# Splitting 640 tokens as 512 and 128 instead of 320 and 320 in the matmuls of a two-layer streaming encoder

## The chip, the core and the metric

The kernel runs on one core of one Trainium2 chip. The metric is device time in microseconds (us) of one launch. The inputs lie in the chip's main memory (HBM) at the start and the outputs lie there at the end.

## What is computed

Two layers of an encoder trunk, for 512 prompt tokens and, with the same weights, for 128 stream tokens (8 streams of 16). All data is float32. Cut to what matters:

```
def half_ffn(x, norms, w_gu, w_down):
    h = rms_norm(x, norms[0])
    g, u = jnp.split(h @ w_gu, 2, axis=-1)
    return x + 0.5 * rms_norm((jax.nn.silu(g) * u) @ w_down, norms[1])
...
def trunk_layer(x, past, ...):
    x = half_ffn(x, norm_ffn1, ffn1_w_gate_up, ffn1_w_down)
    m, st = token_mixer(rms_norm(x, norm_mix[0]), past, w_in, w_out, ...)
    x = x + rms_norm(m, norm_mix[1])
    x = half_ffn(x, norm_ffn2, ffn2_w_gate_up, ffn2_w_down)
```

The model width is 1024 and the hidden width of each FFN 2816. `token_mixer` holds a projection `h @ w_in`, sparse attention, a gated recurrence, a convolution, and a projection `mix @ w_out`. The change touches only the matmuls with the large weights (`w_gu`, `w_down`, `w_in`, `w_out`), the sum of squares behind `rms_norm`, and the instructions that read their results.

## The kernel before

**Layout.** Activations lie with channels on the 128 partitions and all 640 tokens along the free axis: tokens 0 to 511 are the prompt, 512 to 639 the streams. `x`, `y`, `hr`, `hid` and `proj` are cut into pieces of 128 channels by 640 tokens.

**A product in three.** Each float32 operand of a large matmul is split into a high part, rounded to the type `float32r`, and the rest, also `float32r`. `three` (L287 to L292) then issues three matmuls into one PSUM region, high times high, high weights times low activations, and low weights times high activations. Every matmul brings its own load of 128 x 128 weights into TensorE, so each matmul has one LDWEIGHTS. All of them show in the profile as L291.

**Two token parts.** A PSUM bank holds 512 float32 per partition, so 640 tokens need two. `product_tile` calls `three` twice: bank `4j+2c` takes tokens 0 to 319 and bank `4j+2c+1` tokens 320 to 639 (`HALF` is 320). `j` is 0 or 1 and alternates, so one half of the eight banks is filled while the other is read.

**The stages.** For each layer: `ffn` (first), `projections`, a mixer (`select_and_recur`, `attend`) that the change doesn't touch, `output_projection`, and `ffn` (second). `pair_of_tiles` computes two tiles of 128 output channels over 8 pieces of input channels, which is 8 x 2 x 2 x 3 = 96 matmuls; in `ffn` `down_tile` computes one tile over 12 or 10 pieces. A `Lead` opens each `ffn` and `projections`: DVE scales and adds the preceding result to `x` and splits it (L387, L384, L407), piece by piece. The first `pair_of_tiles` waits for each of the 8 pieces (`split`), with 12 matmuls to a piece. `ones_sum` (L316) adds squares over the channels by a matmul in plain float32 against a matrix of ones.

**What runs beside.** SP loads the weights into `stage` (L270), ACT rounds the high part into `wr` (L282), DVE subtracts for the low part (L286). DVE reads the PSUM results (L548, L550 for gate and up; L563, L565 for down; L621, L622, L626, L627 and L630 for the projection; L692 for the output projection). Each such read covers both banks as a view of 2 x 320 elements; `halves` gives its counterpart in SBUF the same shape. Semaphores join the engines: `w_lo` says that weights are ready, `evac` that PSUM has been read, `used` that a tile is complete.

Of the kernel before, what the change touches and what calls it, by code (L numbers as in the profile page):

```python
# [22 lines left out]
ALU = mybir.AluOpType  # L23
# [5 lines left out]
TOK = SEQ + NS * LS  # L29
# [34 lines left out]
def build(nc, ins, outs):  # L64
    stack = ExitStack()
    with stack:
# [5 lines left out]
        def sem(name, once=False):  # L72

            s = stack.enter_context(nc.semaphore(name))
            if not once:
                all_sems.append(s)
            return s
# [75 lines left out]
        def halves(view):  # L153

            return view.rearrange("p (a n) -> p a n", a=2)

        stored = sem("stored")
        par_in = sem("par_in")

# [134 lines left out]
        def product_tile(pe, j, k, c, width, size, v, start, stop):  # L294

            at_ = k * size + 128 * c
            for a in range(2):
                mm = three(pe, ps[:, 4 * j + 2 * c + a, 0:HALF], lambda s: wr[:, j, s, at_:at_ + 128],
                           lambda t: v[:, t, k, a * HALF:(a + 1) * HALF], start, stop)
            return mm  # L300

        def pair_of_tiles(pe, i, j, n0, width=2, split=None):
# [10 lines left out]
        def ones_sum(pe, bank, view, done):  # L313

            for a in range(2):
                mm = pe.matmul(ps[:, bank + a, 0:HALF], ones[:], view[:, a * HALF:(a + 1) * HALF],  # L316
                               start=True, stop=True)
            mm.then_inc(done, 1)

        class Lead:  # L320
# [48 lines left out]

            def act_norm(self, act):  # L370
                act.wait_ge(self.total, 1)
                act.activation(halves(rs), ps[:, 4:6, 0:HALF], ACT.Sqrt, bias=EPS, scale=1.0 / D).then_inc(self.root, 1)

            def pool_part(self, pool):
                pool.wait_ge(self.y_total, 1)
# [43 lines left out]
        def ffn(l, tag, n0, wgu, wd, lead, first, after, ahead):  # L419
# [17 lines left out]
            with nc.Block() as block:  # L437
# [92 lines left out]
                @block.vector  # L530
                def _(dve):
                    if n0 == 0:
                        dve.wait_ge(par_in, 16)
                        dve.wait_ge(x_in, 16)
                        dve.sem_inc(evac, 2)
                        split_lo(dve, 0, 0, 0)
                    lead.dve_part(dve)
                    lead.dve_norm(dve)
                    rs2 = halves(rs)
                    if n0 == 0:  # L540
                        dve.wait_ge(table_out, 16)
                    dve.sem_inc(hid_ready, 1)
                    for f0, nf, gu, dn in chunks:
                        with dve.Fori(0, nf // 2) as i:
                            for j in range(2):
                                dve.wait_ge(used, i * 2 + (gu + j + 1))
                                dve.wait_ge(hid_ready, i * 2 + (f0 + j + 1))
                                dve.tensor_tensor(halves(sg[:, 0]), ps[:, 4 * j:4 * j + 2, 0:HALF], rs2,  # L548
                                                  ALU.mult).then_inc(g_scaled, 1)
                                dve.tensor_tensor(halves(sg[:, 1]), ps[:, 4 * j + 2:4 * j + 4, 0:HALF], rs2,  # L550
                                                  ALU.mult).then_inc(evac, 1)
                                dve.wait_ge(evac, i * 2 + (gu + j + 3))
                                dve.wait_ge(silu, i * 2 + (f0 + j + 1))
                                dve.tensor_tensor(sg[:, 1], sg[:, 0], sg[:, 1], ALU.mult).then_inc(hid_done, 1)  # L554
                                dve.wait_ge(hid_hi, i * 2 + (f0 + j + 1))
                                dve.tensor_tensor(hid_view(i, j, 1), sg[:, 1], hid_view(i, j, 0).bitcast(F32),  # L556
                                                  ALU.subtract).then_inc(hid_ready, 1)
                                split_lo(dve, i, j, gu + 2)
                        def down_tile(i, j, split):
                            dve.wait_ge(used, i * 2 + (dn + j + 1))  # L560
                            src = ps[:, 4 * j:4 * j + 2, 0:HALF]
                            if f0 == 0:
                                dve.tensor_copy(halves(yv[:, i, j, :]), src).then_inc(evac, 1)  # L563
                            else:
                                dve.tensor_tensor(halves(yv[:, i, j, :]), halves(yv[:, i, j, :]), src,  # L565
                                                  ALU.add).then_inc(evac, 1)
                            if split:
                                split_lo(dve, i, j, dn + 2)
                        last = bool(f0)
                        with dve.Fori(0, KD // 2 - last) as i:  # L570
                            for j in range(2):
                                down_tile(i, j, True)
                        if last:
                            down_tile(KD // 2 - 1, 0, ahead)
                            down_tile(KD // 2 - 1, 1, False)


        def projections(l, lead):
            w = ins["w_in"].rearrange("l (i j) p n -> l i j p n", j=2)
            pv = proj[:].rearrange("p (i j c) n -> p i j c n", j=2, c=2)  # L580
            NU = 12

            with nc.Block() as block:
                @block.sync
                def _(sp):
                    load_pairs(sp, PROJ + 2, NU - 2, lambda i, j: w[l, i + 1, j])

                @block.tensor
                def _(pe):
                    lead.pe_start(pe)  # L590
                    pair_of_tiles(pe, 0, 0, PROJ, split=lead.split)
                    lead.pe_norm(pe)
                    pair_of_tiles(pe, 0, 1, PROJ)
                    with pe.Fori(0, NU // 2 - 2) as i:
                        for j in range(2):
                            pair_of_tiles(pe, i, j, PROJ + 2)
                    for j in range(2):
                        pair_of_tiles(pe, NU // 2 - 1, j, PROJ, 2 - j)

                @block.scalar  # L600
                def _(act):
                    lead.act_part(act)
                    lead.act_norm(act)
                    with act.Fori(0, NU // 2 - 1) as i:
                        for j in range(2):
                            act.wait_ge(used, i * 2 + (PROJ + j + 1))
                            split_hi(act, i, j, PROJ + 2)

                @block.gpsimd
                def _(pool):  # L610
                    lead.pool_part(pool)

                @block.vector
                def _(dve):
                    lead.dve_part(dve)
                    lead.dve_norm(dve)
                    rs2 = halves(rs)
                    with dve.Fori(0, NU // 2 - 1) as i:
                        for j in range(2):
                            dve.wait_ge(used, i * 2 + (PROJ + j + 1))  # L620
                            dve.tensor_tensor(halves(pv[:, i, j, 0, :]), ps[:, 4 * j:4 * j + 2, 0:HALF], rs2, ALU.mult)  # L621
                            dve.tensor_tensor(halves(pv[:, i, j, 1, :]), ps[:, 4 * j + 2:4 * j + 4, 0:HALF], rs2,  # L622
                                              ALU.mult).then_inc(evac, 1)
                            split_lo(dve, i, j, PROJ + 2)
                    dve.wait_ge(used, OUTP - 1)
                    dve.tensor_tensor(halves(pv[:, NU // 2 - 1, 0, 0, :]), ps[:, 0:2, 0:HALF], rs2, ALU.mult)  # L626
                    dve.tensor_tensor(halves(pv[:, NU // 2 - 1, 0, 1, :]), ps[:, 2:4, 0:HALF], rs2,  # L627
                                      ALU.mult).then_inc(evac, 1)
                    dve.wait_ge(used, OUTP)
                    dve.tensor_tensor(halves(pv[:, NU // 2 - 1, 1, 0, :]), ps[:, 4:6, 0:HALF], rs2,  # L630
                                      ALU.mult).then_inc(evac, 1)


        def output_projection(l):
# [4 lines left out]
            with nc.Block() as block:  # L639
# [40 lines left out]
                def _(dve):  # L680
# [7 lines left out]
                    for s in range(4):  # L688
                        dve.wait_ge(used, OUTP + s + 1)
                        j = s % 2  # L690
                        for c in range(2):
                            cp = dve.tensor_copy(halves(y[:, 2 * s + c]), ps[:, 4 * j + 2 * c:4 * j + 2 * c + 2, 0:HALF])  # L692
                        cp.then_inc(evac, 1)
                        if s < 3:
                            split_lo(dve, s // 2, s % 2, OUTP + 2)
# [1022 lines left out]
```

## Time and profile before

| | us |
|---|---|
| time of three executions, median | 3253.17 |
| lowest, highest | 3252.92, 3257.25 |
| span of the profiled execution | 3254.3 |
| PE (matmuls) busy | 2851.5 |
| PEld (weight loads) busy | 2665.5 |
| DVE busy | 1528.1 |
| ACT busy | 944.0 |
| POOL busy | 476.2 |

The profiled execution has no time of its own beside its span. The span lies within the range of the three times and 1.1 us above their median, so a difference worked out on the span is applied to either alike. PE and PEld are the same engine, TensorE: matmuls and weight loads overlap, and their mean durations overlap with those of their neighbours too. So "mean ns" of one matmul is its latency, and what one costs in a stream is busy time divided by count. A plain float32 matmul stands in the trace as two records, each with a load.

### The profile page before, as it was taken

What the parts mean: (1) busy time and instruction counts of PE and PEld (TensorE: products, weight loads), DVE (VectorE), ACT (ScalarE), POOL (GpSimd) and SP (SyncE); (2) the same over time, 40 slices, a digit from 0 to 9 for tenths busy, and PEclk for the clock granted to TensorE, in tenths of its full rate; (3) what the DMA queues carried; (4) which work ended last, traced back from release to release, by engine and by line L of the source; (5) the groups of instructions that cost most, each with busy time, mean ns of one, the idle gap of its engine ahead of it and who ended that gap; (6) DMA issues with size and microseconds to landing.
All of it is one profiled execution on the core that took longest, in us unless ns stands there. A gap on an engine that the chain in (4) does not pass through costs nothing. (4 is left out here: it accounts for less than half of the span.)

```text
span 3254.3 us, 44093 instructions
## 1 busy us (share of the span) xinstructions
PE 2851.5 (88%) x18054; PEld 2665.5 (82%) x18054; DVE 1528.1 (47%) x1886; ACT 944.0 (29%) x1237; POOL 476.2 (15%) x328
## 2 busy tenths in 40 slices
PE   1999998997477979999969999989955788999997
PEld 1899998894354879999969999979834458999997
DVE  1633333528965353333353333352499644433333
ACT  1322223216423332212232212231362342322221
POOL 1100001105812120000120000020084313000001
PEclk9999999998768989999989999999976798999998
DMA  5122212113010212122112122122120111212211
GB/s 108 65 71 71 78 63 79 65 52 98 1 73 7 72 52 78 59 83 73 57 60 84 62 81 77 57 73 78 36 76 15 59 46 46 78 68 75 78 61 63
DMA packets 50676, 209.51 MB, mean 64 GB/s; under 512 B 13928, under 2 KB 14312, under 8 KB 34568
## 3 DMA queue, kind: packets, MB, share of 16 engines
q1 hardware_dynamic: 50568, 208.05, 19.3%
q8 instruction: 70, 1.15, 0.1%
q14 instruction: 38, 0.31, 0.0%
HBM read 197.85 MB, written 10.19 MB: 64 GB/s over the span
## 5 line engine op out<-in xcount | busy, mean ns | idle before, releaser
L291 PE MATMUL ps<-hr,wr 128*128 128x320 f32 x11424 | 1707.5, 311 | 83.6 <-DVE hr L407 65.7
L291 PEld LDWEIGHTS ps<-hr,wr 128*128 128x128 f32 x11424 | 1692.3, 189 | 99.7 <-DVE hr L407 43.5
L291 PE MATMUL ps<-hid,wr 128*128 128x320 f32 x4224 | 620.8, 309 | 0.0
L291 PEld LDWEIGHTS ps<-hid,wr 128*128 128x128 f32 x4224 | 619.8, 188 | 0.0
L286 DVE TENSOR_TENSOR wr<-stage,wr 128x2048 fp32r<-128x2048 f32 x184 | 421.7, 2292 | 299.7 <-ACT wr L282 299.7
L282 ACT ACTIVATE wr<-stage 128x2048 fp32r<-128x2048 f32 x184 | 350.6, 1905 | 557.5 <-PE ps L291 288.9
L548 DVE TENSOR_TENSOR arena<-ps,arena 128x640 f32<-128x640 f32 x88 | 72.5, 824 | 545.5 <-PE ps L291 543.8
L523 POOL TENSOR_TENSOR arena<-arena 128x640 f32<-128x640 f32 x28 | 44.3, 1582 | 1737.0 <-ACT arena L499 1737.0
L490 ACT ACTIVATE arena<-arena 128x640 f32<-128x640 f32 x88 | 65.1, 739 | 801.8 <-DVE arena L548 801.8
L860 POOL TENSOR_TENSOR proj<-proj,arena 128x640 f32<-128x640 f32 x120 | 200.1, 1669 | 33.6 <-ACT arena L1018 16.9
L938 PE MATMUL ps<-proj 128*128 128x256 f32 x264 | 90.9, 519 | 97.5 <-issue 78.4
L938 PEld LDWEIGHTS ps<-proj 128*128 128x128 f32 x264 | 70.2, 273 | 117.5 <-issue 82.1
L556 DVE TENSOR_TENSOR hid<-arena,hid 128x640 f32 x88 | 72.6, 825 | 91.8 <-ACT hid L492 91.8
L1017 ACT ACTIVATE arena<-arena,par 128x512 f32<-128x512 f32 x120 | 86.5, 721 | 79.6 <-POOL proj L860 79.6
L380 POOL TENSOR_TENSOR arena<-arena 128x640 f32<-128x640 f32 x48 | 95.6, 1992 | 85.9 <-ACT arena L367 82.4
L563 DVE COPY arena<-ps 128x640 f32 x32 | 26.4, 825 | 164.0 <-PE ps L291 164.0
L621 DVE TENSOR_TENSOR proj<-ps,arena 128x640 f32 x20 | 16.5, 825 | 171.6 <-PE ps L291 171.0
L1428 ACT ACTIVATE arena<-arena 128x128 f32<-128x128 f32 (+4 forms) x80 | 47.7, 596 | 154.4 <-DVE arena L1486 154.4
L492 ACT ACTIVATE hid<-arena 128x640 f32 x88 | 65.1, 740 | 92.7 <-DVE arena L554 92.7
L336 PE MATMUL ps<-ones,arena 128*128 128x1 f32 x70 | 17.6, 320 | 84.7 <-DMA par<-in_params 66.4
L336 PEld LDWEIGHTS ps<-ones,arena 128*128 128x128 f32 x70 | 16.2, 286 | 87.3 <-DMA par<-in_params 67.9
L499 ACT ACTIVATE arena<-arena 128x640 f32 (+1 forms) x32 | 23.6, 739 | 196.3 <-DVE arena L565 196.3
(204 smaller groups left out, 2224.5 us busy)
## 6 DMA issues: line engine op xcount, KB each, us to landing
stage<-in_wgu SPq DMA_DIRECT2D x88, 1024.0 KB, 4.8
stage<-in_wd SPq DMA_DIRECT2D x32, 768.0 KB, 4.2
stage<-in_w_in SPq DMA_DIRECT2D x24, 1024.0 KB, 4.8
stage<-in_wd SPq DMA_DIRECT2D x32, 640.0 KB, 3.8
stage<-in_w_out SPq DMA_DIRECT2D x8, 1024.0 KB, 5.0
arena<-in_ic SPq DMA_DIRECT2D x16, 256.0 KB, 2.8
hf<-bias_table SPq DMA_DIRECT2D x2, 2048.0 KB, 10.7
arena<-in_kc SPq DMA_DIRECT2D x16, 256.0 KB, 5.2
```

Of the source, the lines that this page charges most:

```text
L282: act.activation(wr[:, j, 0], stage[:, j], ACT.Copy).then_inc(w_hi, 1)
L286: dve.tensor_tensor(wr[:, j, 1], stage[:, j], wr[:, j, 0].bitcast(F32), ALU.subtract).then_inc(w_lo, 1)
L291: mm = pe.matmul(out, w(s), v(t), start=start and n == 0, stop=stop and n == 2)
L380: pool.tensor_tensor(ssum, ssum, sqb[:, k % 2], ALU.add).then_inc(self.summed, 1)
L490: act.activation(sg[:, 0], sg[:, 0], ACT.Silu).then_inc(silu, 1)
L492: act.activation(hid_view(i, j, 0), sg[:, 1], ACT.Copy).then_inc(hid_hi, 1)
L548: dve.tensor_tensor(halves(sg[:, 0]), ps[:, 4 * j:4 * j + 2, 0:HALF], rs2, ALU.mult).then_inc(g_scaled, 1)
L556: dve.tensor_tensor(hid_view(i, j, 1), sg[:, 1], hid_view(i, j, 0).bitcast(F32), ALU.subtract).then_inc(hid_ready, 1)
L860: pool.tensor_tensor(yc[:, g], yc[:, g], product[:, n % 3], ALU.add).then_inc(tap_added, 1)
L938: mm = pe.matmul(ps[:, n % 8, 256 * g:256 * g + 256], kp[:, g, 128 * t:128 * t + 128], qz[:, g, :, 128 * t:128 * t + 128], start=True, sto ...
L1017: act.activation(outs_[0], srcs[0], ACT.Identity, scale=tap, bias=bias)
L1428: act.activation(pb[:, u % 3, 0:keys], pb[:, u % 3, 0:keys], ACT.Exp, scale=-1.0, bias=low[:, u:u + 1], accum_out=norm[:, u:u + 1]).then_i ...
```

## The change

The first token part of each product has 512 tokens (the prompt) and the second 128 (the streams). The first fills a whole bank, and the second starts at the next bank, so that the 640 results of a tile lie in one unbroken run. The instructions that read them (on DVE, and the one square root on ACT) take this run as 640 elements in place of 2 x 320. The number of matmuls, of loads, of semaphores and of DMAs stays as it was.

```diff
+        PART = (SEQ, TOK - SEQ)
+
+        def tokens(bank):
+
+            return flat(ps[:, bank:bank + 2])[:, 0:TOK]
...
             for a in range(2):
-                mm = three(pe, ps[:, 4 * j + 2 * c + a, 0:HALF], lambda s: wr[:, j, s, at_:at_ + 128],
-                           lambda t: v[:, t, k, a * HALF:(a + 1) * HALF], start, stop)
+                mm = three(pe, ps[:, 4 * j + 2 * c + a, 0:PART[a]], lambda s: wr[:, j, s, at_:at_ + 128],
+                           lambda t: v[:, t, k, a * SEQ:a * SEQ + PART[a]], start, stop)
...
-                mm = pe.matmul(ps[:, bank + a, 0:HALF], ones[:], view[:, a * HALF:(a + 1) * HALF],
+                mm = pe.matmul(ps[:, bank + a, 0:PART[a]], ones[:], view[:, a * SEQ:a * SEQ + PART[a]],
...
-                act.activation(halves(rs), ps[:, 4:6, 0:HALF], ACT.Sqrt, bias=EPS, scale=1.0 / D).then_inc(self.root, 1)
+                act.activation(rs, tokens(4), ACT.Sqrt, bias=EPS, scale=1.0 / D).then_inc(self.root, 1)
...
-                    rs2 = halves(rs)
+                    rs2 = rs
...
-                                dve.tensor_tensor(halves(sg[:, 0]), ps[:, 4 * j:4 * j + 2, 0:HALF], rs2,
+                                dve.tensor_tensor(sg[:, 0], tokens(4 * j), rs2,
                                                   ALU.mult).then_inc(g_scaled, 1)
...
-                            src = ps[:, 4 * j:4 * j + 2, 0:HALF]
+                            src = tokens(4 * j)
...
-                            cp = dve.tensor_copy(halves(y[:, 2 * s + c]), ps[:, 4 * j + 2 * c:4 * j + 2 * c + 2, 0:HALF])
+                            cp = dve.tensor_copy(y[:, 2 * s + c], tokens(4 * j + 2 * c))
```

The other reads on DVE (L550, L563, L565, L621 to L630) change in the same way.

TensorE's instructions before, around the first `ones_sum` of an `ffn` (L316); L291 is the three-fold product, and the numbers are rows by columns of the moving operand:

```order
L343 MATMUL ps<-cst,tok_r 128x128 x5
L291 MATMUL ps<-hr,wr 128x320 x96
L316 MATMUL ps<-arena,ones 128x320 x2
L291 MATMUL ps<-hr,wr 128x320 x96
L459 UNCONDITIONAL_BRANCH
```

The same place with the change, from the end of the first 96 products into the second (line numbers are 6 higher):

```order
L297 MATMUL ps<-hr,wr 128x512 x3
L297 MATMUL ps<-hr,wr 128x128 x3
L322 MATMUL ps<-arena,ones 128x512
L322 MATMUL ps<-arena,ones 128x128
L297 MATMUL ps<-hr,wr 128x512 x3
L297 MATMUL ps<-hr,wr 128x128 x3
```

Nothing has moved: where 96 equal matmuls stood, 16 groups of three wide and three narrow ones alternate, which is 96 again.

## Rows read from the trace of the kernel before

**Rows 1.** The page: busy us by engine; PE and its clock, tenths in 40 slices

```profile
PE 2851.5 (88%) x18054; PEld 2665.5 (82%) x18054; DVE 1528.1 (47%) x1886; ACT 944.0 (29%) x1237; POOL 476.2 (15%) x328
...
PE   1999998997477979999969999989955788999997
...
PEclk9999999998768989999989999999976798999998
```

**Rows 2.** Groups by line: busy us, mean ns, idle before and releaser

```profile
L291 PE MATMUL ps<-hr,wr 128*128 128x320 f32 x11424 | 1707.5, 311 | 83.6 <-DVE hr L407 65.7 <-DVE hr L685 12.3 <-ACT arena L372 4.8
L291 PEld LDWEIGHTS ps<-hr,wr 128*128 128x128 f32 x11424 | 1692.3, 189 | 99.7 <-DVE hr L407 43.5 <-issue 35.9 <-DVE wr L286 12.5
L291 PE MATMUL ps<-hid,wr 128*128 128x320 f32 x4224 | 620.8, 309 | 0.0
L291 PEld LDWEIGHTS ps<-hid,wr 128*128 128x128 f32 x4224 | 619.8, 188 | 0.0
```

**Rows 3.** Busy time by stretch: us and (count) per engine, granted PE clock, DMA

```profile
280.00:400.00 120.00, 120.00 (x820) 120.00 (x819) 38.31 (x29) 23.24 (x16) 0.00 (x0) 1.00 0.24 82
1900.00:2100.00 200.00, 200.00 (x1366) 200.00 (x1365) 73.68 (x62) 45.59 (x38) 3.16 (x2) 1.00 0.21 71
```

**Rows 4.** Timeline of a tile in the first FFN, all engines

```profile
454.72 15.56 PE L291 MATMUL ps<-hr,wr 128*128 128x320 f32 x105
...
457.80 0.82 DVE L548 TENSOR_TENSOR arena<-ps,arena 128x640 f32<-128x640 f32 x1 [6.56 <-PE ps L291]
...
463.02 2.29 DVE L286 TENSOR_TENSOR wr<-stage,wr 128x2048 fp32r<-128x2048 f32 x1 [0.83 <-ACT wr L282]
```

**Rows 5.** Groups by line in 558.1 to 560.6: matmuls of one column

```profile
L336 PE MATMUL ps<-ones,arena 128*128 128x1 f32 x10 | 1.8, 249 | 1.9 <-PEq L437 1.9
L337 PEld LDWEIGHTS ps<-ones,arena 128*128 128x128 f32 x10 | 1.5, 192 | 0.0
```

**Rows 6.** Timeline of the same stretch: start us, us, pairs of records

```profile
558.17 0.35 PE L336 MATMUL ps<-ones,arena 128*128 128x1 f32 x2 [1.94 <-PEq L437]
...
560.17 0.36 PE L337 MATMUL ps<-ones,arena 128*128 128x1 f32 x2
```

**Rows 7.** Timeline of PEld after a wait: first one load, then two together

```profile
96.55 0.19 PEld L291 LDWEIGHTS ps<-hr,wr 128*128 128x128 f32 x1 [1.93 <-DVE hr L407]
...
96.55 0.30 PEld L291 LDWEIGHTS ps<-hr,wr 128*128 128x128 f32 x2 [1.93 <-DVE hr L407]
```

**Rows 8.** Groups by line, shapes apart: loads of the transposes (L873)

```profile
L873 PEld LDWEIGHTS ps<-cst,proj 128*128 128x128 f32 x40 | 4.3, 141 | 2.8 <-issue 2.8
```

**Rows 9.** Timeline of PE in the first Lead, pieces of 12 matmuls

```profile
90.01 2.02 PE L291 MATMUL ps<-hr,wr 128*128 128x320 f32 x12 [1.66 <-DVE hr L407]
92.86 2.03 PE L291 MATMUL ps<-hr,wr 128*128 128x320 f32 x12 [0.83 <-DVE hr L407]
96.56 2.02 PE L291 MATMUL ps<-hr,wr 128*128 128x320 f32 x12 [1.67 <-DVE hr L407]
99.41 4.13 PE L291 MATMUL ps<-hr,wr 128*128 128x320 f32 x24 [0.83 <-DVE hr L407]
```

**Rows 10.** Who PE waited for: us in total, times, longest

```profile
PE ps L291 <- DVE hr L407: 65.7, 33, 5.7
```

**Rows 11.** Groups by line: DVE and ACT instructions of 640 elements

```profile
L554 DVE TENSOR_TENSOR arena<-arena 128x640 f32<-128x640 f32 x88 | 72.6, 825 | 12.7 <-ACT arena L490 0.2
L548 DVE TENSOR_TENSOR arena<-ps,arena 128x640 f32<-128x640 f32 x88 | 72.5, 824 | 545.5 <-PE ps L291 543.8 <-DVEq L542 1.7
L372 ACT ACTIVATE arena<-ps 128x640 f32<-128x640 f32 x6 | 4.2, 704 | 24.7 <-PE ps L316 24.7
```

**Rows 12.** The plain float32 sums: groups by line, then one in the timeline

```profile
L316 PE MATMUL ps<-arena,ones 128*128 128x320 f32 x24 | 7.4, 431 | 0.0
L316 PEld LDWEIGHTS ps<-arena,ones 128*128 128x128 f32 x24 | 4.3, 188 | 1.0
...
592.73 1.24 PE L316 MATMUL ps<-arena,ones 128*128 128x320 f32 x4
```

More of the change, by code:

```diff
@@ L547, in _ @@
                                 dve.wait_ge(hid_ready, i * 2 + (f0 + j + 1))
-                                dve.tensor_tensor(halves(sg[:, 0]), ps[:, 4 * j:4 * j + 2, 0:HALF], rs2,
+                                dve.tensor_tensor(sg[:, 0], tokens(4 * j), rs2,
                                                   ALU.mult).then_inc(g_scaled, 1)
-                                dve.tensor_tensor(halves(sg[:, 1]), ps[:, 4 * j + 2:4 * j + 4, 0:HALF], rs2,
+                                dve.tensor_tensor(sg[:, 1], tokens(4 * j + 2), rs2,
                                                   ALU.mult).then_inc(evac, 1)
@@ L560, in down_tile @@
                             dve.wait_ge(used, i * 2 + (dn + j + 1))
-                            src = ps[:, 4 * j:4 * j + 2, 0:HALF]
+                            src = tokens(4 * j)
                             if f0 == 0:
-                                dve.tensor_copy(halves(yv[:, i, j, :]), src).then_inc(evac, 1)
+                                dve.tensor_copy(yv[:, i, j, :], src).then_inc(evac, 1)
                             else:
-                                dve.tensor_tensor(halves(yv[:, i, j, :]), halves(yv[:, i, j, :]), src,
+                                dve.tensor_tensor(yv[:, i, j, :], yv[:, i, j, :], src,
                                                   ALU.add).then_inc(evac, 1)
@@ L616, in _ @@
                     lead.dve_norm(dve)
-                    rs2 = halves(rs)
+                    rs2 = rs
                     with dve.Fori(0, NU // 2 - 1) as i:
@@ L620, in _ @@
                             dve.wait_ge(used, i * 2 + (PROJ + j + 1))
-                            dve.tensor_tensor(halves(pv[:, i, j, 0, :]), ps[:, 4 * j:4 * j + 2, 0:HALF], rs2, ALU.mult)
-                            dve.tensor_tensor(halves(pv[:, i, j, 1, :]), ps[:, 4 * j + 2:4 * j + 4, 0:HALF], rs2,
+                            dve.tensor_tensor(pv[:, i, j, 0, :], tokens(4 * j), rs2, ALU.mult)
+                            dve.tensor_tensor(pv[:, i, j, 1, :], tokens(4 * j + 2), rs2,
                                               ALU.mult).then_inc(evac, 1)
@@ L625, in _ @@
                     dve.wait_ge(used, OUTP - 1)
-                    dve.tensor_tensor(halves(pv[:, NU // 2 - 1, 0, 0, :]), ps[:, 0:2, 0:HALF], rs2, ALU.mult)
-                    dve.tensor_tensor(halves(pv[:, NU // 2 - 1, 0, 1, :]), ps[:, 2:4, 0:HALF], rs2,
+                    dve.tensor_tensor(pv[:, NU // 2 - 1, 0, 0, :], tokens(0), rs2, ALU.mult)
+                    dve.tensor_tensor(pv[:, NU // 2 - 1, 0, 1, :], tokens(2), rs2,
                                       ALU.mult).then_inc(evac, 1)
                     dve.wait_ge(used, OUTP)
-                    dve.tensor_tensor(halves(pv[:, NU // 2 - 1, 1, 0, :]), ps[:, 4:6, 0:HALF], rs2,
+                    dve.tensor_tensor(pv[:, NU // 2 - 1, 1, 0, :], tokens(4), rs2,
                                       ALU.mult).then_inc(evac, 1)
```

## The prediction

> **What bounds the kernel now.** I first read the busy shares on the page: TensorE's matmuls cover 2851.5 us of 3254.3, DVE 1528.1 [rows 1]. That alone doesn't make TensorE the bound, so I went to the groups by line. The two groups of L291 hold 15,648 of the 18,054 matmul records and 1707.5 + 620.8 = 2328.3 us, and the engine stood idle only 83.6 us before them [rows 2]. The table of stretches shows the same from within: 820 matmuls fill 120.00 us of 120.00, later 1366 fill 200.00 of 200.00, at a granted clock of 1.00 [rows 3], which is the 2.4 GHz level. In the timeline of a tile DVE waits 6.56 us for PE before it reads PSUM and its last piece of work there ends about 7.5 us after that read began, well inside the 14 us that the next 96 matmuls take [rows 4]. So in these stages nothing but TensorE's own pace sets the time: each nanosecond per matmul appears in the total, 15,648 times.
>
> **What one matmul costs, and why.** The mean of 309 ns [rows 2] is a latency. The pace is 620.8 us / 4224 = 147.0 ns. At one column per clock, 320 columns take 133.3 ns at 2.4 GHz, so about 14 ns come on top. The reader should see beside it that PEld has one load to each matmul and is as busy as PE: the loads lie under the matmuls. The question of the change is how long a load keeps the loading path, because a narrow matmul offers less cover.
>
> Two rows bear on that. First, matmuls of a single column, each with a load of 128 x 128: from the first pair at 558.17 to the last at 560.17 there are 18 records, so 2.00 / 18 = 111 ns each, though one column is next to no work [rows 6]. There the load sets the pace. These loads have a mean of 191 to 192 ns [rows 5] against 188 for L291's [rows 2]; loads of the same shape for transposes (L873) read 141 [rows 8]. So L291's are of the slow kind. Second, L291's own loads after a wait: one load lasts 0.19 us, two together 0.30 [rows 7], so the second began 0.11 us after the first, when nothing but the first load held it up. Both also say that issuing an LDWEIGHTS and a MATMUL takes no more than 111 ns. This gives **111 ns as the floor of a float32r matmul with its own load**, however few columns it has. At 320 columns (147 ns) the floor is hidden; at 128 it isn't.
>
> Here a rule of the Trainium skill would say otherwise. The page "TensorE: Matmul & The Clock Gate", section "Back-to-back issue gap", gives the isolated gap as columns over the clock plus 2.5 ns: 56 ns for 128 columns and 216 for 512, together 272 ns where two of 320 cost 294, which would make this change a gain. The trace doesn't agree with it for these operands, by 147 against 136 ns at 320 columns. The same page says in "LDWEIGHTS (loading the stationary operand)" that a load of 128 columns takes 107 ns, and the trace agrees within 4 ns; by that the gap formula can't hold at 128 columns with a load to each.
>
> **The change part by part.**
>
> *Wide matmul, 512 columns.* 133.3 ns become 213.3. If the 14 ns on top are a fixed cost per matmul, it takes 227 ns; if they grow with the columns, 147.0 x 1.6 = 235; if they vanish, about 216: the four plain float32 records of 320 columns take (1.24 - 0.43) / 3 = 270 ns each [rows 12], which is two passes of 133.3 and 3 ns, so 3 ns on top is the least that a row shows. I take 227.
>
> *Narrow matmul, 128 columns.* The work is 53.3 ns, with the 14 on top 67, and the load 111. The larger sets the pace: 111. Upper bound: the load's 111 and the 14 on top of it, 125. Lower bound for a load that binds: 0.30 - 0.19 = 0.11, so 107 to 111 with the rounding; I take 109.
>
> *Sum.* One wide and one narrow: 227 + 111 = 338 ns, against 2 x 147 = 294, so **+44 ns per pair**. There are 15,648 / 2 = 7824 pairs. The ends are 216 + 109 = 325 (+31) and 235 + 125 = 360 (+66).
>
> *What is hidden.* In the six Leads, PE waits for DVE between pieces, 33 times and 65.7 us in total [rows 10], with gaps of 0.83 to 1.67 us after each 12 matmuls [rows 9]. Six pairs make 6 x 44 = 0.26 us more per piece, less than the smallest gap, and DVE's chain doesn't depend on PE there. I count six covered pieces in each of six Leads: 36 x 6 = 216 pairs cost nothing. Without that cover they would cost 10 us. That leaves 7608 pairs: 7608 x 44 = 335 us.
>
> *The reads of PSUM and the rest.* DVE's read of 2 x 320 from PSUM takes 824 ns; its instruction on one run of 640 in SBUF takes 825 [rows 11]. The shape of the view costs nothing now, so one run can give nothing back; and DVE waits for PE before it (543.8 us in all [rows 11]), so a few ns either way would be hidden. The square root on ACT, 6 times at 704 ns [rows 11], stays. The sums in plain float32 keep 1280 streamed columns per sum: two records each of 320 and 320 become 512 and 128, and at 128 the load's 111 ns stand where the two passes would need 107, so all 24 records [rows 12] cost at most 0.1 us more. Nothing waits longer for weights: ACT, DVE and SP get more time per tile. The mixer stages between have no changed instruction.
>
> Total: 3254.3 + 335 = 3589 us on the profiled span; the median is 1.1 us lower. I say **3590**. The range of this case alone goes from 7608 x 31 = 236 to 7608 x 66 = 502: 3490 to 3756.
>
> **Rivals.**
>
> *A. The narrow matmul runs at plain float32's rate.* No float32r matmul in this trace has fewer than 320 columns, so that its fast rate holds at 128 isn't shown. A plain float32 matmul is two records of two passes each; for 128 columns that is 2 x (2 x 53.3 + 3) = 219 ns by the pace of L316 [rows 12], and 2 x 111 = 222 by the floor of the loads. Then a pair costs 227 + 222 = 449, +155: 7608 x 155 = 1179, and a little of the cover in the Leads is used up (0.93 us per piece against gaps of 0.83 to 1.67). About 4435 us. For it speaks only that nothing excludes it; against it, that the work is the same instruction, one record, with another length.
>
> *B. The load needs 147 ns in float32r.* The 147 ns at 320 columns could be the load's own floor rather than 133 + 14. Then the wide costs 216 and the narrow 147: 363, +69, so 3254 + 525 = 3779. Against it: the second load after a wait begins after 0.11 us [rows 7].
>
> *C. Not slower: the load is covered after all.* This would be so if the loads could run ahead by more than one place, those of the three narrow matmuls under the three wide ones. Then the pace is work alone: 227 + 67 = 294, no change, 3254 us; with 3 ns on top in place of 14, 216 + 56 = 272, and 3254 - 7608 x 0.022 = 3087. The gap formula of the Trainium skill quoted above would give this lower figure. It decides from the point where a load takes under 67 ns or two loads can be held in waiting. Against it are the single-column matmuls at 111 ns [rows 6]: nothing ran ahead there.
>
> *D. The clock falls.* TensorE's granted clock was 1.00 in the long stretches [rows 3]. With narrow matmuls the array streams 640 columns (267 ns) in 338 ns, 79% of the time against 91%. If the clock fell to 1.2 GHz in such stretches, wide and narrow would cost at least 427 (512 columns) and about 213 (twice the load's 107), 640 ns, and the whole would go over 5800 us. In the slices of the page it fell where PE was busy half of the time, and stayed up where it was busy throughout [rows 1]. I give it 1 in 100.
>
> **How the numbers follow.** My forecast (load-bound narrow matmul) 0.81; A 0.10; B 0.04; C 0.04; D 0.01. The likeliest case gives 3590. Its own range, 3490 to 3756, is stretched at the top to take in B: 3490 to 3790. Outside lie A, C and D (0.15) and a little of my own case. Faster by more than 0.2% (6.5 us, about what a measurement of this kernel can tell from no change): 0.02, half of C. Within 0.2%: 0.02. Slower: 0.96.
>
> **What would show it.** In the profile after, the pace of the stretches: groups by line must show wide and narrow forms of L297, 7824 each, with busy times that sum to about 2328 + 340 = 2670 us, and the stretch 280 to 400 us should hold about 120 / 0.169 = 710 matmuls in place of 820. PEld's mean stays at 188 ns. DVE L554 (L548 before) stays at 824 ns, and waits longer for PE. PE's idle time before L297 for DVE's L413 falls by about 10 us. Wrong would be: 820 matmuls in that stretch (C), 530 (A), or a granted clock under 0.9 there (D). The weakest step is the narrow matmul's 111 ns, inferred from matmuls of one column in plain float32.

## The result and the profile after

The changed kernel takes 3627.11 us (median of 4 executions, 3625.75 to 3631.11) against 3253.13 for the kernel before in the same series. The ratio is 1.1143, with a 95% interval from 1.1127 to 1.1159. The forecast was 3590 us, in a range from 3490 to 3790. The loss is 374 us where 337 had been forecast.

On the page of the changed kernel each engine has as many instructions as before, and DVE, ACT and POOL are busy as long as before, to within 1 us. PE's matmuls are busy 380 us longer and the weight loads 52 us ([rows 1] has the line of before).

```profile
span 3623.6 us, 44093 instructions
...
PE 3231.3 (89%) x18054; PEld 2717.6 (75%) x18054; DVE 1527.7 (42%) x1886; ACT 944.3 (26%) x1237; POOL 475.6 (13%) x328
...
PEclk9999999999769899999989999999976898999998
```

The groups by line, with shapes kept apart, answer to [rows 2]. The idle time stands last.

```profile
L297 PE MATMUL ps<-hr,wr 128*128 128x512 f32 x5712 | 1741.7, 413 | 75.4 <-DVE hr L413 58.4 <-DVE hr L691 12.3 <-ACT arena L378 4.8
L297 PEld LDWEIGHTS ps<-hr,wr 128*128 128x128 f32 x11424 | 1730.0, 191 | 329.9 <-issue 35.9 <-DVE hr L413 27.9 <-DVE wr L292 12.5
L297 PE MATMUL ps<-hr,wr 128*128 128x128 f32 x5712 | 850.9, 258 | 0.0
...
L297 PEld LDWEIGHTS ps<-hid,wr 128*128 128x128 f32 x4224 | 633.2, 190 | 90.2
...
L554 DVE TENSOR_TENSOR arena<-ps,arena 128x640 f32<-128x640 f32 x88 | 72.5, 824 | 742.3 <-PE ps L297 740.6 <-DVEq L548 1.7
```

The wide and the narrow matmuls overlap in their records, so the busy times of the two forms add up to more than the stream. With both forms in one group, the view has 1983.5 us for `hr` and 724.1 us for `hid`, 2707.6 in all, where the prediction had about 2670. The pace has to be read from stretches. These are the same two stretches as in [rows 3]:

```profile
280.00:400.00 120.00, 120.00 (x703) 105.05 (x702) 30.43 (x21) 18.62 (x11) 0.00 (x0) 1.00 0.20 69
1900.00:2100.00 200.00, 200.00 (x1170) 175.03 (x1170) 64.40 (x57) 43.75 (x37) 0.00 (x0) 1.00 0.17 61
```

PE is still busy throughout and its clock still granted in full, but 1170 matmuls fit where 1366 did: 170.9 ns each in place of 146.4. The loads were busy without a gap and now leave 25 us of 200 free, although the engine is slower. That is the mark of the new limit: under each wide matmul the loading path stands idle for a part, and under each narrow one it is the array that waits.

The single loads show it directly. Where nothing waits for weights, a load's record begins 2 to 4 ns after the record of the matmul that it lies under. So the distance between the starts of two loads is read here as the cost of one matmul, and over six it gives the same 1026 ns as the stretch. Each of these lines comes from a narrow window that holds one load alone; the first is the load under a group's third wide matmul, the next three are those under its three narrow ones:

```profile
300.45 0.19 PEld L297 LDWEIGHTS ps<-hid,wr 128*128 128x128 f32 x1
300.68 0.19 PEld L297 LDWEIGHTS ps<-hid,wr 128*128 128x128 f32 x1
300.79 0.19 PEld L297 LDWEIGHTS ps<-hid,wr 128*128 128x128 f32 x1
300.90 0.19 PEld L297 LDWEIGHTS ps<-hid,wr 128*128 128x128 f32 x1
301.01 0.19 PEld L297 LDWEIGHTS ps<-hid,wr 128*128 128x128 f32 x1
```

The wide matmul takes 0.23 us and each narrow one 0.11. The trace keeps starts to the nanosecond: from 280 to 400 us the wide ones take 232 ns, and the three narrow ones of a group 108, 111 and 112.

24.5 ns on 15,216 matmuls (those outside DVE's waits, by the count of the prediction) are 373 us. The spans differ by 369.3.

The timeline of the first Lead shows what is hidden. It answers to the second and third line of [rows 9] (L413 is L407 of before): a piece of 12 matmuls became about 0.25 us longer, and the gap before it, behind DVE, shorter by as much.

```profile
91.97 2.27 PE L297 MATMUL ps<-hr,wr 128*128 128x512 f32 x12 [0.57 <-DVE hr L413]
95.66 2.27 PE L297 MATMUL ps<-hr,wr 128*128 128x512 f32 x12 [1.42 <-DVE hr L413]
```

### The profile page after: what moved, and what is told of

Its sections match the earlier page's. It is cut to its first block and busy times, and to the rows that moved or that the text cites. A ratio compares the mean times of both kernels' runs of the same rounds, so it can differ in the third digit from the quotient of the medians.

```text
span 3623.6 us, 44093 instructions
## 1 busy us (share of the span) xinstructions
PE 3231.3 (89%) x18054; PEld 2717.6 (75%) x18054; DVE 1527.7 (42%) x1886; ACT 944.3 (26%) x1237; POOL 475.6 (13%) x328
## 5 line engine op out<-in xcount | busy, mean ns | idle before, releaser
L297 PE MATMUL ps<-hr,wr 128*128 128x128 f32 (+1 forms) x11424 | 1983.5, 336 | 75.4 <-DVE hr L413 58.4
L297 PEld LDWEIGHTS ps<-hr,wr 128*128 128x128 f32 x11424 | 1730.0, 191 | 329.9 <-issue 35.9
L297 PE MATMUL ps<-hid,wr 128*128 128x512 f32 (+1 forms) x4224 | 724.1, 333 | 0.0
L297 PEld LDWEIGHTS ps<-hid,wr 128*128 128x128 f32 x4224 | 633.2, 190 | 90.2
L571 DVE TENSOR_TENSOR arena<-arena,ps 128x640 f32 (+1 forms) x32 | 26.3, 821 | 143.5 <-PE ps L297 143.5
```

The lines of the kernel that those rows point to most:

```text
L297: mm = pe.matmul(out, w(s), v(t), start=start and n == 0, stop=stop and n == 2)
```

## The experiments

The theory: TensorE fetches one matmul's weights under the matmul before it, this takes 107 to 111 ns for 128 x 128 in `float32r`, and a matmul of 128 columns is too short to cover it. The rivals: the reads matter; the order of short matmuls matters; a float32r matmul of few columns is slow by itself; unequal parts have a price of their own. All kernels were timed against the kernel before on the same chip, which took 3256.77 us beside the first four and 3254.82 over all runs beside the last four.

### One run of 640, parts equal

This kernel has the new reads without the uneven split. The first part is put at the end of its bank and the second at the start of the next, so that the readers still find one unbroken run. `FIRST` is 320. The diffs of this section are against the changed kernel; the matmuls of `ones_sum` move to `PLACE` in the same way.

```diff
-        PART = (SEQ, TOK - SEQ)
+        FIRST = 320
+        PART = (FIRST, TOK - FIRST)
+        PLACE = (slice(512 - FIRST, 512), slice(0, TOK - FIRST))
...
-            return flat(ps[:, bank:bank + 2])[:, 0:TOK]
+            return flat(ps[:, bank:bank + 2])[:, 512 - FIRST:512 - FIRST + TOK]
...
-                mm = three(pe, ps[:, 4 * j + 2 * c + a, 0:PART[a]], lambda s: wr[:, j, s, at_:at_ + 128],
-                           lambda t: v[:, t, k, a * SEQ:a * SEQ + PART[a]], start, stop)
+                mm = three(pe, ps[:, 4 * j + 2 * c + a, PLACE[a]], lambda s: wr[:, j, s, at_:at_ + 128],
+                           lambda t: v[:, t, k, a * FIRST:a * FIRST + PART[a]], start, stop)
```

> Half of the change alone: both token parts keep 320 columns, but the first is put at the end of its bank and the second at the start of the next, so that the readers take one run of 640. Theory (the loss is all in the narrow matmul, whose own load of weights keeps it at 111 ns or more; the reads cost what they did): pace 147 ns per matmul, DVE's read 824 ns, 3253 us within 0.2%. Rival (the reads on one run cost or give something of their own): away from 3253 by more than 0.2%.

Measured: 3257.01 us, ratio 0.9999 (0.9990 to 1.0008). The stretch of 200 us holds as many matmuls as in [rows 3]:

```profile
1900.00:2100.00 200.00, 200.00 (x1366) 200.00 (x1365) 73.71 (x62) 45.57 (x38) 3.16 (x2) 1.00 0.20 71
```

The new reads cost and give nothing, to within 0.1%. The whole loss lies in the split.

### Wide and narrow in turn

```diff
-            for a in range(2):
-                mm = three(pe, ps[:, 4 * j + 2 * c + a, 0:PART[a]], lambda s: wr[:, j, s, at_:at_ + 128],
-                           lambda t: v[:, t, k, a * SEQ:a * SEQ + PART[a]], start, stop)
+            for n, (s, t) in enumerate(((0, 0), (0, 1), (1, 0))):
+                for a in range(2):
+                    mm = pe.matmul(ps[:, 4 * j + 2 * c + a, 0:PART[a]], wr[:, j, s, at_:at_ + 128],
+                                   v[:, t, k, a * SEQ:a * SEQ + PART[a]], start=start and n == 0,
+                                   stop=stop and n == 2)
```

> 512 and 128 columns, but wide and narrow matmuls alternate (w n w n w n) in place of w w w n n n. Theory (one load at a time, fetched under the matmul before it and 107 to 111 ns long): each narrow matmul still covers one load, so six matmuls take 3 x 230 + 3 x 111 = 1026 ns as in the changed kernel, 3627 us. Rival (the loss comes from three short matmuls in a row, which drain what was loaded ahead): a narrow one between two wide ones is covered, six take about 880 ns, 3254 us.

Measured: 3610.80 us, ratio 1.1084 (1.1067 to 1.1101).

```profile
1900.00:2100.00 200.00, 200.00 (x1179) 175.92 (x1178) 64.35 (x56) 43.74 (x37) 0.00 (x0) 1.00 0.18 61
```

The pace is 169.6 ns; six matmuls take 1018 ns, where a covered narrow one would have given 880. A narrow matmul between two wide ones is exposed just as one of three in a row. This kernel is 0.45% faster than the changed one, which the theory doesn't give. The starts of single loads in the two traces show where the difference lies: every narrow matmul takes 108 ns here, and 108, 111 and 112 ns in groups of three; the wide ones take 232 in both. That is some 7 ns per six matmuls, 17 us on the 2536 groups outside DVE's waits, where 16 were measured. Why the second and the third load of a group last longer stays open.

This trace also shows that loading the same weights twice running is not skipped. The first narrow matmul of three covers a load of the block that is already in use, the second and third a load of another block, and all of them take 108 ns.

### Split as 384 and 256, as 352 and 288, as 448 and 192

Only `FIRST` differs from the first experiment.

> Split as 384 and 256, one run of 640. From 147 ns at 320 columns and 230 at 512 a matmul costs 7 ns and 0.437 ns per column. Theory (a floor of 111 ns): 175 + 119 = 293 ns for the two, nothing is under the floor, 3254 us, within 0.3%. Rival A (float32r is slower per column below 256 columns): 256 is not below, the same. Rival B (any unequal split pays a fixed price of about 50 ns per narrow matmul): 3254 + 7608 x 0.050 = about 3630 us.

> Split as 448 and 192. Theory (floor): the wide one 202.5 ns, the narrow one would need 91 and is kept at 111.5, together 314, +21 ns on each of 7608 pairs: 3411 us. Rival A (below 256 columns each column costs 111.5 / 128 = 0.87 ns): the narrow one takes 167, together 370, +76: 3836 us. Rival B (a fixed price for unequal parts): about 3630 us.

> Split as 352 and 288. 384 and 256 cost 0.77% though 119 ns is above the floor of 111. Theory 1 (that loss comes from 256 columns being so close to the floor that a little unevenness of the load exposes it): at 288 columns (133 ns) it is gone, 3254 us within 0.2%. Theory 2 (the loss goes with the inequality of the parts): half of it stays, about 3267 us.

Measured: 384 and 256 take 3282.89 us, ratio 1.0077 (1.0061 to 1.0092); 448 and 192 take 3408.88 us, ratio 1.0468 (1.0452 to 1.0484); 352 and 288 take 3256.19 us, ratio 1.0000 (0.9991 to 1.0009). The same stretch in the three kernels, in this order:

```profile
1900.00:2100.00 200.00, 200.00 (x1355) 200.00 (x1354) 72.36 (x62) 44.96 (x37) 1.57 (x1) 1.00 0.20 70
```

```profile
1900.00:2100.00 200.00, 200.00 (x1278) 191.17 (x1278) 63.44 (x51) 39.59 (x30) 0.00 (x0) 1.00 0.21 72
```

```profile
1900.00:2100.00 200.00, 200.00 (x1365) 200.00 (x1365) 73.80 (x63) 46.42 (x40) 3.15 (x2) 1.00 0.21 72
```

The reader should look at the loads' busy time: 200.00 while both parts stay over the floor, and less than 200 as soon as the narrow one falls under it. At 448 and 192 the floor's forecast was 3411 us and the two rivals' 3836 and 3630. That excludes a slow rate below 256 columns and a fixed price for unequal parts. At 384 and 256 a loss of 26 us came that the theory had not forecast: 147.6 ns per matmul in place of 146.4. At 352 and 288 it is gone. So it doesn't go with inequality as such, and it fits a narrow matmul (119 ns) so close to the floor that the load is exposed in part. That last step is argued, not shown. The trace of 384 and 256 adds that the loss isn't the same in every stage. In the second `ffn` of the first layer the same instructions run at 148.7 ns:

```profile
1300.00:1500.00 200.00, 200.00 (x1345) 200.00 (x1344) 68.84 (x57) 43.77 (x34) 0.00 (x0) 1.00 0.22 74
```

The starts of single loads show two regular patterns, each repeated every six matmuls: the narrow ones take 118, 121 and 121 ns from 1900 us on, and 127, 118 and 125 from 1300 us on. It is a steady slowdown and not a chance one, and what picks the pattern stays open. At 448 and 192, which lies under the floor, the pace is the same 156.5 ns in both stretches.

### Shorter loads under the same narrow matmuls

```diff
-            for a in range(2):
-                mm = three(pe, ps[:, 4 * j + 2 * c + a, 0:PART[a]], lambda s: wr[:, j, s, at_:at_ + 128],
-                           lambda t: v[:, t, k, a * SEQ:a * SEQ + PART[a]], start, stop)
+            mm = three(pe, ps[:, 4 * j + 2 * c, 0:SEQ], lambda s: wr[:, j, s, at_:at_ + 128],
+                       lambda t: v[:, t, k, 0:SEQ], start, stop)
+            for n, (s, t, m) in enumerate(((0, 0, 128), (0, 1, 128 if stop else 64), (1, 0, 128 if stop else 64))):
+                mm = pe.matmul(ps[0:m, 4 * j + 2 * c + 1, 0:PART[1]], wr[:, j, s, at_:at_ + m],
+                               v[:, t, k, SEQ:TOK], start=start and n == 0, stop=stop and n == 2)
```

> 512 and 128 columns in the order of the changed kernel, but two of the three narrow matmuls take only the first 64 columns of weights (except at the last piece of a tile), so that their loads are half as long; the rest of the products of these two for output channels 64 to 127 of the streams is left out. The matmuls keep their 128 moving columns. Theory (load as floor): the first and second narrow matmul now cover a load of 53 ns and take about 60 ns each, the third still covers a full load, 111; six take 922 ns in place of 1026. 2306 of 2608 groups of six are shortened, some 70 of them under DVE's waits: 3627 - 2234 x 0.104 = about 3395 us. Rival A (a matmul of 128 float32r columns itself takes 111 ns): unchanged, 3627 us.

Measured: 3410.23 us, ratio 1.0473 (1.0457 to 1.0489). That is 217 us less than the changed kernel; the theory had said 232, the rival nothing. By the starts of single loads from 280 us on, the wide matmuls take 234 ns here in place of 232; three of them on 2234 groups are 13 of the 15 us that are missing.

The total alone leaves another rival. The shortened matmuls also write only 64 partitions of PSUM, and they might be faster for that and not for their loads. The trace decides it. In this kernel the loads of wide (L297) and narrow (L306) matmuls have lines of their own, and as above each of these lines comes from a window that holds one load alone. Start and length in us:

```profile
300.54 0.13 PEld L306 LDWEIGHTS ps<-hid,wr 128*64 128x64 f32 x1
300.59 0.14 PEld L306 LDWEIGHTS ps<-hid,wr 128*64 128x64 f32 x1
300.65 0.19 PEld L297 LDWEIGHTS ps<-hid,wr 128*128 128x128 f32 x1
300.76 0.19 PEld L297 LDWEIGHTS ps<-hid,wr 128*128 128x128 f32 x1
```

The first line is the load under the first narrow matmul, the second that under the second, the third that under the third; the fourth lies under the next wide one. The second and the third narrow matmul are the same instruction, 64 weight columns and 128 moving columns. The second has a short load under it and takes 0.06 us, the third a full load and takes 0.11. The groups by line give the two kinds of loads, of 128 and of 64 weight columns:

```profile
L297 PEld LDWEIGHTS ps<-hid,wr 128*128 128x128 f32 x2112 | 344.0, 189 | 31.2
...
L306 PEld LDWEIGHTS ps<-hid,wr 128*64 128x64 f32 x1280 | 124.2, 134 | 28.6
```

The record is 55 ns shorter for half of the columns, which fits a load of about 110 ns with 128 columns and 55 with 64. So the narrow matmul's time is its successor's load.

### The narrow matmul doubled

```diff
+            mm = three(pe, ps[:, 4 * j + 2 * c, 0:SEQ], lambda s: wr[:, j, s, at_:at_ + 128],
+                       lambda t: v[:, t, k, 0:SEQ], start, stop)
+            mm = three(pe, ps[:, 4 * j + 2 * c + 1, 0:256].rearrange("p (b n) -> p b n", b=2),
+                       lambda s: wr[:, j, s, at_:at_ + 128],
+                       lambda t: v[:, t, k, SEQ:TOK].unsqueeze(1).to_broadcast([128, 2, 128]), start, stop)
```

> The narrow matmul takes its 128 columns twice, as 256 columns into 256 places of its bank, the second half never read: twice the streaming work for the streams, with the same load. Theory (floor of 111 ns, own pace at 256 columns 119): only 7 to 8 ns more per narrow matmul, 3627 + 7608 x 0.0075 = 3684 us. Rival C (the narrow matmul pays 0.87 ns per column): 223 ns, 3627 + 7608 x 0.111 = about 4470 us.

Measured: 3688.51 us, ratio 1.1334 (1.1317 to 1.1351), 61 us more than the changed kernel for 7824 times 128 more columns. In the stretch from 280 us on the pace is 120 / 688 = 174.4 ns, 3.6 ns more per matmul than the changed kernel's 120 / 703:

```profile
280.00:400.00 120.00, 120.00 (x688) 105.06 (x687) 30.82 (x22) 18.60 (x11) 0.00 (x0) 1.00 0.22 75
```

At 0.44 ns per column the added work would be 56 ns each, 426 us on the 7608 outside DVE's waits. Six sevenths of it went into time in which the array had stood waiting for weights.

### Equal parts in turn

The loop of the second experiment with the parts and the places of the first (`FIRST` at 320, and `PLACE`).

> 320 and 320 with one run of 640, but first and second part alternate, so that the same weights are loaded twice in a row. Theory (every matmul makes its own load and at 320 columns hides it, in any order): 147 ns, 3254 us within 0.2%. Rival (the alternating order of 512 and 128 was 0.45% faster than the grouped one because the order itself saves about 1 ns per matmul, by reusing the weights' place or by alternating banks): 3254 - 15.6 = about 3238 us.

Measured: 3258.67 us, ratio 1.0008 (1.0000 to 1.0017). No gain beyond the noise: the order is worth nothing where every load is covered. No kernel tried beats the one before.

## Why the prediction was right

**What bounds.** Right. The stretches were full before and after, and the whole difference of the spans, 369.3 us, follows from the pace of 15,216 matmuls to within 4 us. The 374 us are a difference of medians. The prediction took the profiled span of before as 1.1 us above its median time; in the runs that have both, a span lies 2 to 3 us below the time of its own execution (3623.6 beside 3625.75), so that execution took about 3257 us, some 3 to 4 us over the median.

**The narrow matmul, 111 ns.** Right, and it was the step on which the prediction rested. The prediction took it from matmuls of one column in plain float32 and from two loads after a wait, and called it its weakest step. In the trace after, the three narrow ones take 108, 111 and 112 ns. Halved loads, doubled columns and the split of 448 and 192 confirm it: 3395, 3684 and 3411 us were forecast from it, and 3410, 3689 and 3409 came.

**The wide matmul, 227 ns.** This term was too small. Six matmuls take 6 x 170.9 = 1026 ns; three narrow ones at 111 leave 692, which is 231 for a wide one. The single starts say 232, without the 111. The prediction took the 14 ns on top of 133 as fixed per matmul and kept "if they grow with the columns, 235" as the end. The truth lies between, at about 18 ns over 213. With 231, and 146.4 in place of the rounded 147.0 for the kernel before, a pair costs 342 - 293 = +49 ns, and 7608 pairs 373 us. These two corrections make up the 37 us by which the forecast was short.

**What is hidden.** Right in kind: the idle time behind DVE's L413 (L407 before) fell from 65.7 us [rows 10] to 58.4. That is 7 us where 10 had been forecast. At 0.25 us each, 7.3 us are about 29 covered pieces, where 36 had been counted.

**The reads of PSUM.** Right. The read takes 824 ns in both, and alone the change of reads gave a ratio of 0.9999. The plain float32 sums were to grow by 0.1 us at most in all; each grew from 1.24 us [rows 12] to 1.29, which is 0.3 for the six.

**The rivals.** Plain float32's rate for narrow matmuls (A) is excluded by the stretch, 703 matmuls where it would have had about 530; a load of 147 ns (B) by the same count and by the halved loads; covered loads (C) by the alternating order too; a lower clock (D) by 1.00 in the stretches. The gap formula of the Trainium skill's page "TensorE: Matmul & The Clock Gate", section "Back-to-back issue gap", would have given 3087 us. The page gives it for an isolated matmul, which the prediction's working with it leaves aside. The measurement decides against it as the pace of float32r matmuls with a load to each: 170.9 ns on average where it has 136.

Of the signs that the prediction names, two more were off: PEld's mean was to stay at 188 ns and rose to 190 and 191, and the matmuls' busy time was to be about 2670 us and was 2707.6, for the same reason as the total. The stretch from 280 us held 703 matmuls where 710 were forecast.

## What to carry to other kernels

Where each matmul brings its own weights, find out how long a load keeps the loading path before you split the moving columns: for 128 x 128 in float32r it was 108 to 112 ns at the full clock, the work of some 240 columns. Keep every part above that with some room (288 and 352 were free, 256 and 384 cost 0.8%); filling a whole bank gains nothing if it leaves a short rest. A stream can be 100% busy in the profile on both sides of such a change, so count matmuls per stretch, and see whether the loads still run without a gap.

## What the runs showed of the hardware that was not expected

A float32r matmul didn't run at one column per clock plus a fixed cost. At 1.00 granted clock it took 146.4 ns at 320 columns and 231 at 512, so a column costs 84.6 / 192 = 0.44 ns, where 2.4 GHz would be 0.417, and about 5 ns come on top. In the kernel of 352 and 288 single matmuls take 161 and 132 ns, 0.45 ns per column between them. (Its mean of 146.5 ns by itself would fit any straight line, since the two parts add up to 640 in both kernels.) Why a column costs more than a clock is not shown.

Second, three loads in a row behind narrow matmuls took 108, 111 and 112 ns, and single ones between wide matmuls 108 each. That accounts for the 16 us between groups of three and the order in turn; its cause stays open.
